# Second block's feed-forward up projections: both activation parts summed in the same 256 columns, one bank a chunk

## What is computed

```python
def swiglu_ffn(h, w_gu, w_down):
    a, b = jnp.split(h @ w_gu, 2, axis=-1)
    return (jax.nn.silu(a) * b) @ w_down

def second_block(x, ...):
    for l in range(DEPTH):
        h = swiglu_ffn(rmsnorm(x, ffn1_pre_g[l]), ffn1_w_gu[l], ffn1_w_down[l])
        x = x + 0.5 * rmsnorm(h, ffn1_post_g[l])
        h = mixing_sublayer(...)
        x = x + rmsnorm(h, mix_post_g[l])
        h = swiglu_ffn(rmsnorm(x, ffn2_pre_g[l]), ffn2_w_gu[l], ffn2_w_down[l])
        x = x + 0.5 * rmsnorm(h, ffn2_post_g[l])
    return x
```

## Time and profile before

| | |
|---|---|
| median of 3 runs | 1792.0 us (1789.89 to 1793.45) |
| the profiled execution | 1792.04 us, its span 1790.3 us |
| TensorE busy | 1778.8 us, 99% of the span |
| VectorE busy | 1402.9 us, 78% |
| ScalarE busy | 904.5 us, 51% |
| GpSimd busy | 219.7 us, 12% |
| DMA | 357.43 MB, 200 GB/s |

### The profile page before, as it was taken

How to read it: one execution, slowest core, us unless ns; L and a number is a source line. 1 busy time by engine, 2 the same in 40 slices (tenths; PEclk the granted TensorE clock), 3 DMA queues, 4 the chain that set the end, 5 groups by cost and what they waited for, 6 DMA issues and landing times.

```text
span 1790.3 us, 25922 instructions
## 1 busy us (share of the span) xinstructions
PE 1778.8 (99%) x10010; PEld 1588.6 (89%) x10010; DVE 1402.9 (78%) x1599; ACT 904.5 (51%) x998; POOL 219.7 (12%) x189
## 2 busy tenths in 40 slices
PE   9999999999999999999999999999999999999998
PEld 7988998889889898899898888998899898888997
DVE  7897867678869667777779987778777779987776
ACT  5564434445644444644555546444544555546443
POOL 0000000000001000000059230000000058230000
PEclk9999999999999999999999999999999999999999
DMA  9546565555556555655564556555655564555553
GB/s 315 205 157 227 188 212 209 189 215 200 187 215 222 205 196 186 214 197 194 181 204 172 183 210 217 202 196 192 223 199 197 188 203 167 186 212 205 201 197 117
DMA packets 52018, 357.43 MB, mean 200 GB/s; under 512 B 6552, under 2 KB 6688, under 8 KB 10080
## 3 DMA queue, kind: packets, MB, share of 16 engines
q1 hardware_dynamic: 47952, 341.93, 54.1%
q0 software_dynamic: 3696, 14.33, 2.7%
q10 hardware_dynamic: 288, 0.04, 0.0%
HBM read 354.15 MB, written 2.11 MB: 199 GB/s over the span
## 4 chain that ended last, share of the span: by engine, by line
PE 94%; DVE 4%; issue 1%; ACT 1%; DMA 1%; DVEq 0%; POOLq 0%; POOL 0%; SPq 0%; ACTq 0%
PE ps L245 21%; PE ps L327 13%; PE ps L335 13%; PE ps L328 13%; PE ps L251 11%; PE ps L207 3%; PE ps L208 3%; PE ps L209 3%; PE ps L225 2%; PE ps L232 2%; PE ps L226 2%; DVE w_lo L182 1%; PE ps L2917 1%; PE ps L2916 1%; PE ps L2921 1%
## 5 line engine op out<-in xcount | busy, mean ns | idle before, releaser
L182 DVE TENSOR_TENSOR w_lo<-raw,w_hi 128x2048 fp32r<-128x2048 f32 x312 | 717.4, 2305 | 208.4 <-ACT w_hi L175 208.0
L175 ACT ACTIVATE w_hi<-raw 128x2048 fp32r<-128x2048 f32 x312 | 596.1, 1912 | 424.1 <-PE ps L335 168.6
L245 PE MATMUL ps<-a,w_hi 128*128 128x512 f32 x1760 | 398.3, 379 | 0.8 <-ACT w_hi L175 0.8
L245 PEld LDWEIGHTS ps<-a,w_hi 128*128 128x128 f32 x1760 | 329.3, 189 | 46.0 <-ACT w_hi L175 1.2
L327 PE MATMUL ps<-w_hi,a 128*128 128x512 f32 x592 | 226.9, 383 | 0.0
L328 PE MATMUL ps<-w_hi,a 128*128 128x512 f32 x592 | 224.4, 379 | 0.0
L251 PEld LDWEIGHTS ps<-a,w_lo 128*128 128x128 f32 x1760 | 213.6, 192 | 5.9
L327 PE MATMUL ps<-w_hi,mix 128*128 128x512 f32 x576 | 218.7, 380 | 0.0
L328 PE MATMUL ps<-w_hi,mix 128*128 128x512 f32 x576 | 218.3, 379 | 0.0
L251 PE MATMUL ps<-a,w_lo 128*128 128x256 f32 x1760 | 214.2, 275 | 0.0
L335 PE MATMUL ps<-w_lo,a 128*128 128x512 f32 x592 | 139.8, 379 | 0.0
(11 more groups left out here) (416 smaller groups left out, 2267.2 us busy)
## 6 DMA issues: line engine op xcount, KB each, us to landing
raw<-in_w_b SPq DMA_DIRECT2D x198, 1024.0 KB, 4.9
raw<-in_w_a SPq DMA_DIRECT2D x124, 1024.0 KB, 4.9
rows<-in_post_gains POOLq DMA_DIRECT2D x6, 512.0 KB, 5.9
rows<-in_rows_a POOLq DMA_DIRECT2D x2, 1028.0 KB, 8.3
raw<-in_w_a SPq DMA_DIRECT2D x4, 512.0 KB, 7.1
rows<-in_rows_a POOLq DMA_DIRECT2D x2, 1024.0 KB, 6.9
x<-in_x SPq DMA_DIRECT2D x2, 512.0 KB, 6.0
a_gates<-bias_line POOLq DMA_DIRECT2D x2, 512.0 KB, 7.7
```

The lines of the kernel that those rows point to most:

```text
L175: act.activation(k.w_hi[s], k.raw[:, s, :], ACT.Copy).then_inc(k.hi_ready, 1)
L182: dve.tensor_tensor(k.w_lo[s], k.raw[:, s, :], k.w_hi[s].bitcast(F32), ALU.subtract).then_inc(k.lo_ready, 1)
L245: pe.matmul(both, hi[:, kt, n * P:(n + 1) * P], k.a[:, :, kt, :].rearrange("p s (t n) -> p s n t", t=TT), start=kt == 0, stop=False)
```

## The change

The up chunks of units 1 to 10 are computed by `f_chunk` in place of `f_pair`: chunk a into bank 0 (4 for unit 1), chunk b into bank 2 (6 for unit 1). The two reductions of a unit are gone. The product with the norm's factors reads the bank and writes `hid_r`; the product of silu's result with b reads `hid_r` and the bank. The semaphores `asum_ready` and `bsum_ready` are gone: TensorE waits for `scaled_ready` and `gated_ready` instead. In unit 1 the second product now stands ahead of the weight split that it stood behind. `f_pair` and `sum_halves` stay in use in the first block.

```diff
@@ VectorE
                 def scale(j, trips=0, q=0):
                     dve.wait_ge(k.chunk_done, st.results(l, a_chunk(f, j), trips))
-                    r = hid_r[:, j % 2, :].rearrange("p (t n) -> p t n", t=2)
-                    sum_halves(dve, r, k, 4 if j == 1 else 0).then_inc(asum_ready.sem, 1)
+                    r = hid_r[:, j % 2, :].rearrange("p (f n) -> p f n", f=2)
                     if (l, f, j) == (0, 0, 1):
                         dve.wait_ge(rbc_ready.sem, rbc_ready.at(l, 1))
                     elif j == 1:
                         dve.wait_ge(r_spread.sem, r_spread.at(l, 16 + 32 * f))
-                    dve.wait_ge(asum_ready.sem, (l * 2 + f) * (FF_B - 1) + q + j)
-                    dve.tensor_tensor(by_tile(r), by_tile(r), r_tokens, ALU.mult).then_inc(scaled_ready.sem, 1)
+                    dve.tensor_tensor(by_tile(r), tile_pairs(k, 4 if j == 1 else 0), r_tokens, ALU.mult).then_inc(scaled_ready.sem, 1)
...
                     r = hid_r[:, j % 2, :]
-                    sum_halves(dve, hid_b.rearrange("p (t n) -> p t n", t=2), k, 6 if j == 1 else 2)\
-                       .then_inc(bsum_ready.sem, 1)
+                    r_pairs = by_tile(r.rearrange("p (f n) -> p f n", f=2))
+                    dve.wait_ge(silu_ready.sem, n)
+                    dve.tensor_tensor(r_pairs, r_pairs, tile_pairs(k, 6 if j == 1 else 2), ALU.mult).then_inc(gated_ready.sem, 1)
                     if j == 1:
                         split_low(k, dve, st, l, lows[0], trips)
-                    dve.wait_ge(bsum_ready.sem, (l * 2 + f) * (FF_B - 1) + q + j)
-                    dve.wait_ge(silu_ready.sem, n)
-                    dve.tensor_tensor(r, r, hid_b, ALU.mult).then_inc(gated_ready.sem, 1)
@@ TensorE
                     if j >= 2:
-                        pe.wait_ge(asum_ready.sem, (l * 2 + f) * (FF_B - 1) + q + (j - 1))
-                    f_pair(k, pe, a_chunk(f, j), 4 if j == 1 else 0, st.count(l, a_chunk(f, j), trips))
+                        pe.wait_ge(scaled_ready.sem, (l * 2 + f) * (FF_B - 1) + q + (j - 1))
+                    f_chunk(k, pe, a_chunk(f, j), st.count(l, a_chunk(f, j), trips), [4 if j == 1 else 0], [range(KT)], aop)
...
                     if j >= 2:
-                        pe.wait_ge(bsum_ready.sem, (l * 2 + f) * (FF_B - 1) + q + (j - 1))
-                    f_pair(k, pe, b_chunk(f, j), 6 if j == 1 else 2, st.count(l, b_chunk(f, j), trips))
+                        pe.wait_ge(gated_ready.sem, base + j)
+                    f_chunk(k, pe, b_chunk(f, j), st.count(l, b_chunk(f, j), trips), [6 if j == 1 else 2], [range(KT)], aop)
...
                     if j == 0:
-                        pe.wait_ge(asum_ready.sem, (l * 2 + f) * (FF_B - 1) + 1)
+                        pe.wait_ge(scaled_ready.sem, (l * 2 + f) * (FF_B - 1) + 1)
...
                 def wait_first_b():
-                    pe.wait_ge(bsum_ready.sem, (l * 2 + f) * (FF_B - 1) + 1)
+                    pe.wait_ge(gated_ready.sem, (l * 2 + f) * FF_B + 2)
```

More of the change, by code:

```diff
@@ L1720, in second_block @@
         conv_part = sig("conv_part", 1)
-        asum_ready, bsum_ready = (sig(n, 2 * (FF_B - 1)) for n in ("asum_ready", "bsum_ready"))
-        hid_b = GU[:, 2 * 512:3 * 512]
         scaled_ready, uv_done = sig("scaled_ready", 2 * (FF_B - 1)), sig("uv_done", 1)
```

## The result

The change takes 1801.73 us (median of 4 runs, 1801.16 to 1802.74) against 1791.7 us before (4 runs). The ratio is 1.0058, 95% interval 1.0046 to 1.0070: slower by 10 us. The forecast was 1802.0, slower.

What follows compares the result with a forecast made beforehand. TensorE, busy 1778.8 of 1790.3 us, was taken to bound the kernel. Extra passes +10.0, VectorE's saving 0 and waits 0, on 1792.0 us, gave 1802.0 us, range 1798.5 to 1805.5.

Steps and rivals of the forecast that it cites:

- Part 1: TensorE, high half of the second block's up chunks: two 256-column passes per 512-column one, +0.125 us a chunk, +10.0 us.
- rival A: Not slower: extra passes cost almost nothing, +3.4 us, 1795.4 us, if a narrow pass steps under 109.5 ns; chance 4%.
- Part 2: VectorE's reductions go and its products read the banks: 97 us off VectorE, worth nothing on the path.
- Part 3: TensorE's waits for products instead of reductions: cost 0; tightest in the first feed-forward's first unit, margin 0.4 us.
- C: Slower still: product waits of 0.2 us a chunk, +14 us, or 1 us a loop jump, +12, 1814; chance 4%.
- D: The first unit's handover waits in all four feed-forwards by one product (0.8 us): +3.2 us, 1805.2 us; chance 5%.

## Why the prediction was right

**Part 1, the extra passes: right in size, and the reason was not known.** It priced a chunk from `f_chunk` as it already ran, 5.36 against 5.235 us, and took 80 x 0.125 = 10.0 us. Measured: 5.36 us a chunk, and by units 0.24 us for two chunks, 9.6 us in all. The other 0.4 us were rounding of the starts; that the medians differ by exactly 10.0 us is luck within their scatter, and the span is 9.5 us longer. What decided was to look for the very form that the change uses, and to price it by starts. The rule of the Trainium skill, page "TensorE: Matmul & The Clock Gate", section "Back-to-back issue gap" (columns plus 2.5 ns), by which the sum was +3.2 us, is the price of the passes alone: it is the 3.2 us that the run with 64 weight columns leaves. It misses the price here because it holds only while a pass is longer than its own weight load. The same section of the Trainium skill says so in part: it calls the rule the gap of an isolated pass, without the weight load, and says that in a stream of loads and passes both set the spacing. The prediction's "whatever its length" left that out. The prediction rejected the rule on the row and had nothing to put in its place; rival A had the condition right (a step under 109.5 ns), and its case needs fewer weight columns.

**Part 2, VectorE: right on the path, and its size partly by luck.** It named 97 us, measured 95.6 (1402.9 to 1307.3), worth nothing on the path; 1.0003 in the run with that side alone. Both products were priced too dear. The second was taken as 800 ns and measured 686, at the level of the old SBUF product (693); the first was taken as 758 and measured 743. The groups alone fell by 102.0 us (97.9 + 33.5 + 27.7 before, 29.7 + 27.4 after). VectorE's busy time fell by less, in part because neighbouring instructions overlap at their ends by some hundredths of a microsecond; the rest was not taken apart. Nothing in the forecast hung on it.

**Part 3, the waits: right but for a margin.** The prediction said that the second product of the first unit would leave 0.4 us. It left nothing. VectorE's and TensorE's timelines there, after the change:

```profile
732.86 0.69 DVE L2326 TENSOR_TENSOR GU<-GU,ps 128x512 f32<-128x512 f32 x1 [3.06 <-ACT GU L2039]
```

```profile
733.32 0.38 PE L328 MATMUL ps<-w_hi,mix 128*128 128x512 f32 x1
733.60 0.48 PE L327 MATMUL ps<-w_hi,mix 128*128 128x512 f32 x1
733.92 0.38 PE L328 MATMUL ps<-w_hi,mix 128*128 128x512 f32 x1
```

The product ends at 733.55, and the pass that needs it starts at 733.60; the steps 0.28 and 0.32 stand where 0.22 is the rule, 0.17 us lost, once. The step that failed is the use of times from before on both sides of the difference: in this execution TensorE came 0.44 us earlier to this place (`down(0)` at 731.81, 732.25 before) instead of 0.25 later, since it had waited 0.3 us for its input at the start where it was 1.2 before. Silu came only 0.29 us earlier (732.13, 732.42 before); ScalarE had waited 0.99 us for a weight chunk's DMA ahead of it, 0.71 before. A margin of a few tenths between an engine and a chain that begins with a DMA was no margin here. A wait as short as this is not in TensorE's list, so the list can't rule it out for the other feed-forwards; the lag can: it grew there by 2.41, 2.40 and 2.40 us, which is what ten units at 0.24 give. Rivals C and D did not come: no wait in the loop, nothing at the jumps back, and of D's four waits of 0.8 us one of 0.17.

## What to carry to other kernels

Where TensorE is busy without gaps, price an edit by its starts per pass, and look first whether the trace already runs the new form somewhere. Keep the moving side of a pass longer than the load of its weights: with 128 fp32r weight columns a pass of 128 to 256 columns cost 111.6 ns in these runs, so 512 columns in one pass cost 216 ns, in two equal passes 223, in unequal ones 248 and 274, and in four 446. Where single steps alternate, price the whole chunk, since a short pass's loss shows one step late. Work taken from an engine that TensorE does not wait for came back here as that engine's idle time.

## What the runs showed of the hardware that was not expected

- A pass of 128, 192 or 256 columns in a stream with 128 weight columns each costs about the same: 111.6 ns for four of 128; 273.8 - 162.5 = 111.3 and 247.5 - 136.0 = 111.5 ns for 128 and 192 columns beside a longer pass (its own columns plus 2.7 ns taken off); 111.6 for 256. With 64 weight columns 58.2 ns at 128 moving columns and 109.3 at 256.
- Two passes in turn with the same weights gain nothing over different ones, 3.57 us a high half in both orders.
- VectorE's product with the norm's row got faster (838 ns in the mean before, 743 after), and not by reading the bank. Below are its four combinations: operand in SBUF or in the bank, beside passes of 512 or of 256 columns on TensorE. The width of the passes goes with 75 to 100 ns, the place of the operand with 5 ns one way or 20 the other. Why it does so is not shown. In the order of the rows: before (SBUF, 512), passes split only (SBUF, 256), VectorE's side alone (bank, 512), the change (bank, 256).

```profile
L2319 DVE TENSOR_TENSOR GU<-GU,keep 128x512 f32<-128x512 f32 x40 | 33.5, 838 | 1.7
...
L2339 DVE TENSOR_TENSOR GU<-GU,keep 128x512 f32<-128x512 f32 x40 | 30.5, 763 | 1.6
...
L2315 DVE TENSOR_TENSOR GU<-ps,keep 128x512 f32<-128x512 f32 x40 | 33.7, 843 | 35.4 <-PE ps L251 35.1 <-DMA keep<-bias_line 0.2
...
L2315 DVE TENSOR_TENSOR GU<-ps,keep 128x512 f32<-128x512 f32 x40 | 29.7, 743 | 39.7 <-PE ps L232 39.6
```
